# Prompt attentions with one more unit in flight, and output projection weights loaded a stage ahead with longer weight rings

## The chip, the cores and the metric

The kernel runs on one core of a Trainium2 chip. The metric is the device time of one execution in microseconds (us); lower is better. TensorE is called PE here, VectorE DVE, ScalarE ACT, GpSimd POOL and SyncE SP.

## The reference

One decode step of a two-layer decoder, all float32, for a prompt of 256 tokens and 8 sample sequences of 8 tokens each (320 tokens in all, width 1024). Layer 0 mixes by latent attention and dilated window attention, layer 1 by a gated convolution; each layer then attends to a memory and runs a sparse expert layer ("peer"). Cut to what matters:

```
x <- LN(a*x + mixer(x));  x <- LN(a*x + mem_attend(x));  x <- LN(a*x + PEER(x))

def mla_attend(q_pos, q_lat, q_rope, ckv, krope, k_pos):
    s = (einsum(q_lat, ckv) + einsum(q_rope, krope)) * MLA_SCALE      # 8 heads, 256 + 32 features
    p = softmax(where(k_pos <= q_pos, s, -inf)); return einsum(p, ckv)
o_mla = einsum(o_lat, w_uv)                                            # w_uv: 256 x 8 x 64
# window attention: 3 groups of 4 heads of 128; bias = rel_bias[bucket(distance)], softmax, weighted sum
y = concat([o_mla, o_swa]) @ attn_w_out                                # layer 0
y = (b_gate * conv(c_gate * h)) @ conv_w_out                           # layer 1
def mem_attend(x, kv, wq, wo):                                         # 256 memory rows, 4 heads of 256
    s = einsum(x @ wq, k) * MEM_SCALE; return einsum(softmax(s), v) @ wo
```

## The kernel before

The program is a row of stages. Each stage is one `k.block()` (line 182), and all engines meet at its end, so a stage that ends earlier starts the next one earlier. Intermediate results stay in SBUF. SP issues nearly all transfers, on one queue, in the order in which its program has them. Names of tiles begin with the name of their stage.

The stages that the prediction speaks of, in order of time:

- **mlp** (100.6 to 207.2 us): `attend_prompt`, latent attention of the prompt. 16 units of one head and one block of 128 queries: units 0 to 7 have 128 keys, 8 to 15 have 256. The object `BiasByDistance` (lines 1250 to 1290) works beside it: in units 3 to 10 PE makes the window attention's bias by distance (L1281, 15 products with 33 rows and 4 columns of weights), ACT takes them (L1288), and when all 15 are taken SP stores them (L1269) and spreads each of the three groups over 128 rows of DRAM (L1273, 3 transfers of 1 MB).
- **ms** set-up and **mls**: the sample's latent attention. A small stage loads the page table and a mask (L1472, L1473) and waits for both; then `attend_sample` reads page numbers from the table and loads pages.
- **mv** (448.0 to 467.0 us), `mla_values_stage`: loads `w_uv` (0.5 MB, L1224), then 32 matmuls (L1232).
- **swp** (682.5 to 741.5 us): `attend_prompt`, window attention of the prompt; 8 units, 4 with 384 score columns, 4 with 768.
- **nx0** and **nx1**, **nm0** and **nm1**, **nf0**: `joined_stage`. It runs a list of products in units of two weight chunks (1024 x 512, 2 MB each) through a ring of two slots. In nx0 and nx1 the first unit is the mixer's output projection; then a layer norm of the residual runs on DVE while PE makes the memory's keys or values; x is turned (L441) after a given chunk (after chunk 3 in nx0, after chunk 2 in nx1), and the memory queries follow. nm0 and nm1 have the memory's output projection alone.
- **m0p** and **m1p** (44.1 and 44.6 us): `attend_prompt`, memory attention of the prompt; 8 units of 256 keys. Then **m0s** and **m1s**, the sample's, which stream 1 MB pieces of the memory cache.
- **c_**: `odd_mixer`, the convolution on DVE, between nf0 and nx1.
- **peer** (p0e, p1e): about 815 us each; not touched.

In `attend_prompt` one unit passes through these steps: scores on PE (L664), bias or copy, maximum and scale on DVE (L700 or L703, L705, L706: `maxima`), exponential on ACT (L735), division on DVE (L712, L713: `finish`), transposes on PE (L673), their copy to `pT` on ACT (L747), the product with the values on PE (L679), and its copy out on DVE (L719: `take`). Scores have two PSUM buffers; `pT` has one. The orders are written out by hand:

```
PE,  unit u:  scores(u+1); bias products; transposes(u), wait for pT, values(u)
DVE, unit u:  finish(u); maxima(u+1); take(u)
ACT, unit u:  exps(u+1); bias copies; copy of pT(u)
```

So between the transposes of unit u and its values PE waits until ACT has done `exps(u+1)`, which itself waits for `maxima(u+1)`, and the copy.

In `joined_stage` a chunk's load waits until the chunk two before it is done (`wait(sp, chunk_done, n - 1)`), and PE waits before chunk n for its weights and for `bank_free >= n - 1`, the evacuation of chunk n - 2. With 320 tokens the last 64 are computed for both chunks of a unit together, so both chunks are done, and can be evacuated, only at the unit's end.

Of the kernel before, what the change touches and what calls it, by code (L numbers as in the profile page):

```python
# [16 lines left out]
P = 128  # L17
# [88 lines left out]
class Kernel:  # L106


    def __init__(self, nc, ctx, io):
# [5 lines left out]
        self.window_stored = ctx.enter_context(nc.semaphore("window_stored"))  # L115
        self.mem_kv_stored = ctx.enter_context(nc.semaphore("mem_kv_stored"))
# [221 lines left out]
def joined_stage(k, name, out_job, norm, mid=(), last=(), turn_at=0, memT=None):  # L338
# [12 lines left out]
    with ExitStack() as ctx:  # L351
        ring = k.sb(ctx, name + "_w", [P, 2, KC * 512])
# [4 lines left out]
        w_landed = [k.sem(f"{name}_w_landed{s}") for s in range(2)]  # L357
# [14 lines left out]
        def slot_view(s, kc, chunk):  # L372
            return ring[:, s, 0:kc * chunk].rearrange("p (c n) -> p c n", c=kc)

        @block.sync
        def _(sp):
            def load(n):
                (_, aT, w, chunk, _), i = units[n // 2]
                src = w[:, (2 * i + n % 2) * chunk:(2 * i + n % 2 + 1) * chunk].rearrange("(c p) n -> p c n", p=P)
                wait(sp, chunk_done, n - 1)  # L380
                sp.dma_start(slot_view(n % 2, aT.shape[1], chunk), src).then_inc(w_landed[n % 2], 16)
# [9 lines left out]
            for n in range(2 * len(units)):  # L391
                load(n)
                if n == 1 and out_job:
                    load_norm()

        @block.tensor
        def _(pe):
            def product(u, between):
# [3 lines left out]
                for s in range(2):  # L402
                    n = 2 * u + s
                    pe.wait_ge(w_landed[s], 16 * (u + 1))
                    wait(pe, bank_free, n - 1)
                    wv = slot_view(s, kc, chunk)
# [14 lines left out]
                if paired:  # L421
                    j, (t0, rows) = len(parts(kind, aT, chunk)) - 1, parts(kind, aT, chunk)[-1]
                    for c in range(kc):
                        for s in range(2):
                            mm = pe.matmul(k.ps[64 * s:64 * s + 64, 4 * s + j, 0:chunk], aT[:, c, t0:t0 + rows],
                                           slot_view(s, kc, chunk)[:, c, :], start=(c == 0), stop=(c == kc - 1))
# [201 lines left out]
def attend_prompt(k, name, units, cols, scale, mask_scales, beside=None):  # L628
# [3 lines left out]
    with ExitStack() as ctx:  # L632
        s = k.sb(ctx, name + "_s", [P, 2, cols])
        p = k.sb(ctx, name + "_p", [P, 2, cols])
        pT = k.sb(ctx, name + "_pT", [P, cols // P, P])
# [23 lines left out]
        def _(pe):  # L659
# [8 lines left out]
            def values(u):  # L668
# [5 lines left out]
                mm.then_inc(turned, 1)  # L674
                pe.wait_ge(pT_ready, u + 1)
                wait(pe, o_taken, u - 1)
                for b in range(len(units[u]["outs"])):
                    for j, (_, vs) in enumerate(keys):
                        mm = pe.matmul(k.ps[:, 6 + u % 2, b * P:(b + 1) * P], vs[b], pT[:, j, :],  # L679
                                       start=(j == 0), stop=(j == len(keys) - 1))  # L680
                mm.then_inc(o_ready, 1)

            scores(0)
            for u in range(U):
                if u + 1 < U:
                    scores(u + 1)
                if beside:
                    beside.tensor(pe, u)
                values(u)

        @block.vector
        def _(dve):
# [30 lines left out]
            for u in range(U):  # L723
# [3 lines left out]
                take(u)  # L727

        @block.scalar
        def _(act):  # L730
# [20 lines left out]
def attend_sample(k, name, a):  # L751
# [7 lines left out]
    with ExitStack() as ctx:  # L759
# [32 lines left out]
        def _(sp):  # L792
# [27 lines left out]
            repeat_ends(sp, PAIRS, body)  # L820

# [392 lines left out]
def mla_values_stage(k, e):  # L1214

    nc, io = k.nc, k.io
    with ExitStack() as ctx:
        wuv = k.sb(ctx, "mv_wuv", [P, 2, MLA_H, D_V])
        landed, made, taken = k.sem("mv_landed"), k.sem("mv_made"), k.sem("mv_taken")
        block = ctx.enter_context(k.block())  # L1220

        @block.sync
        def _(sp):
# [152 lines left out]
def even_mixer(k, oT):  # L1376
# [3 lines left out]
    with ExitStack() as ctx:  # L1380
        e = {"oT": oT}
        with ExitStack() as c1:
# [6 lines left out]
            e["mask"] = k.sb(c1, "e_causal", [P, 2, SEQ])  # L1389
            with ExitStack() as c2:  # L1390
# [61 lines left out]
def mla_sample(k, e):  # L1452
    nc, io = k.nc, k.io
    with ExitStack() as ctx:
# [10 lines left out]
        half = PAST // 2  # L1465
        table_landed, masked = k.sem("ms_table_landed"), k.sem("ms_masked")
        with ExitStack() as c2:
# [196 lines left out]
def memory_attention(k, memory):  # L1664
# [790 lines left out]
```

## Time and profile before

| | |
|---|---|
| median of 3 runs | 3481.22 us (3477.48 to 3485.13) |
| the profiled execution | 3498.17 us |
| its span | 3496.4 us |
| busy share PE / DVE / ACT / POOL | 84% / 43% / 16% / 18% |
| prompt attention stages mlp, swp, m0p, m1p | 106.6, 59.0, 44.1, 44.6 us |
| the two peer stages | about 1630 us together |

The profile has one execution: busy time of each engine, the span in 40 slices with TensorE's granted clock in tenths of full speed, groups of instructions by line, and which wait ended each idle time. A window "A:B" is counted in us from the span's start. A matmul of float32 shows two records for each instruction, so "x8" in a row of matmuls is four instructions.

### The profile page before, as it was taken

The page shows a single profiled execution, that of the slowest core. Times are in us where ns is not written, and L with a number is a line of the kernel's source. Part 1 is how long each engine was busy: PE and PEld are TensorE (multiplying, and loading weights), DVE is VectorE, ACT ScalarE, POOL GpSimd, SP SyncE. Part 2 cuts the span into 40 slices and gives each one's busy share as a digit, 9 for nine tenths or more (in the row PEclk, how much of TensorE's full clock was granted, in tenths as well). Part 3 has the DMA queues.
Part 4 walks back from the last instruction along what each step waited for, and adds up shares of the span by engine and source line. Part 5 has one row for each costly group of instructions (what it writes and reads, how often), then busy time and mean ns, then how long its engine had stood idle before and what let it go on. Part 6 is the DMA issues. An engine that isn't in the chain of part 4 may idle for free. (4 is left out here: it accounts for less than half of the span.)

```text
span 3496.4 us, 45163 instructions
## 1 busy us (share of the span) xinstructions
PE 2934.1 (84%) x17313; PEld 2381.8 (68%) x17313; DVE 1509.9 (43%) x3598; ACT 544.2 (16%) x1380; POOL 612.4 (18%) x642
## 2 busy tenths in 40 slices
PE   6867768866669668999989998968678999999997
PEld 3434423554535438999989997644437999989997
DVE  1211100022210225997975553021215997985553
ACT  1223300133301211112100000101221112110000
POOL 0000040000000000433443330000000432443330
PEclk8668889878889789999999999989698999999998
DMA  3349977859842433998989996322343898989995
GB/s 116 108 148 300 316 206 253 280 158 244 206 160 96 162 115 122 355 378 305 348 311 409 409 409 215 121 86 96 121 156 122 318 381 300 349 310 409 408 409 210
DMA packets 275160, 867.70 MB, mean 248 GB/s; under 512 B 30625, under 2 KB 54210, under 8 KB 272423
## 3 DMA queue, kind: packets, MB, share of 16 engines
q1 hardware_dynamic: 198932, 593.14, 48.6%
q0 software_dynamic: 76032, 271.88, 20.6%
q8 instruction: 130, 2.13, 0.3%
q14 instruction: 66, 0.54, 0.0%
HBM read 846.23 MB, written 109.08 MB: 273 GB/s over the span
## 5 line engine op out<-in xcount | busy, mean ns | idle before, releaser
L2271 PE MATMUL ps<-xT,p0e_uT 128*128 128x192 f32 x2048 | 345.9, 328 | 11.1 <-DMA p0e_uT<-in_peer_uT 6.7
L2271 PE MATMUL ps<-xT,p1e_uT 128*128 128x192 f32 x2048 | 345.7, 328 | 9.5 <-DMA p1e_uT<-in_peer_uT 6.4
L2271 PEld LDWEIGHTS ps<-xT,p0e_uT 128*128 128x128 f32 x2048 | 334.0, 191 | 13.9 <-DMA p0e_uT<-in_peer_uT 8.4
L2297 PE MATMUL ps<-p0e_S,p_qT 128*128 128x192 f32 x2048 | 337.3, 327 | 6.3 <-DMA p_qT<-in_peer_v 6.3
L2271 PEld LDWEIGHTS ps<-xT,p1e_uT 128*128 128x128 f32 x2048 | 334.7, 191 | 11.6 <-DMA p1e_uT<-in_peer_uT 7.8
L2297 PE MATMUL ps<-p1e_S,p_qT 128*128 128x192 f32 x2048 | 337.2, 327 | 5.6 <-DMA p_qT<-in_peer_v 5.4
L2297 PEld LDWEIGHTS ps<-p0e_S,p_qT 128*128 128x128 f32 x2048 | 333.1, 190 | 10.4 <-DMA p_qT<-in_peer_v 10.4
L2297 PEld LDWEIGHTS ps<-p1e_S,p_qT 128*128 128x128 f32 x2048 | 332.4, 190 | 10.1 <-DMA p_qT<-in_peer_v 10.0
L2075 DVE SCALAR_TENSOR_TENSOR h_tok<-p1e_rows,p1e_dots,h_tok 128x1024 f32<-128x1024 f32 x127 | 163.1, 1284 | 143.7 <-DMA p1e_rows<-in_peer_v,p1e_expert 125.7
L2075 DVE SCALAR_TENSOR_TENSOR h_tok<-p0e_rows,p0e_dots,h_tok 128x1024 f32<-128x1024 f32 x127 | 163.1, 1284 | 141.3 <-DMA p0e_rows<-in_peer_v,p0e_expert 134.5
L1965 POOL DMA_INDIRECT p0e_rows<-in_peer_u,p0e_expert x128 | 153.4, 1199 | 394.7 <-DVE p0e_dots L2064 207.1
L1965 POOL DMA_INDIRECT p1e_rows<-in_peer_u,p1e_expert x128 | 153.4, 1199 | 393.9 <-DVE p1e_dots L2064 206.9
L1965 POOL DMA_INDIRECT p1e_rows<-in_peer_v,p1e_expert x128 | 127.0, 992 | 195.2 <-DVE h_tok L2075 172.7
L1965 POOL DMA_INDIRECT p0e_rows<-in_peer_v,p0e_expert x128 | 126.1, 985 | 196.4 <-DVE h_tok L2075 174.7
L2064 DVE CUSTOM_DVE_ANT_0 p1e_rows<-p1e_rows,x_tok 128x1024 f32<-128x1024 f32 x128 | 154.9, 1218 | 1.6
L2064 DVE CUSTOM_DVE_ANT_0 p0e_rows<-p0e_rows,x_tok 128x1024 f32<-128x1024 f32 x128 | 154.9, 1218 | 1.6
L844 PE MATMUL ps<-ident,ms_pages 128*128 128x128 f32 (+1 forms) x384 | 70.3, 340 | 64.9 <-DMA ms_pages<-in_cache_mla 60.3
L503 DVE SCALAR_TENSOR_TENSOR x_tok<-x_tok,h_tok 128x1024 f32<-128x1024 f32 (+1 forms) x15 | 17.4, 1218 | 236.9 <-ACT h_tok L471 195.9
L293 PE MATMUL ps<-win_w,xT 128*128 128x512 f32 x192 | 89.9, 630 | 29.3 <-DMA win_w<-in_attn_w_in 29.3
L700 DVE SCALAR_TENSOR_TENSOR swp_s<-ps,e_bias_p 128x384 f32<-128x384 f32 (+1 forms) x8 | 6.1, 757 | 241.2 <-PE ps L664 241.2
L844 PEld LDWEIGHTS ps<-ident,ms_pages 128*128 128x128 f32 (+1 forms) x384 | 48.1, 155 | 86.7 <-DMA ms_pages<-in_cache_mla 37.6
L2288 PE MATMUL ps<-h_tok 128*128 128x128 f32 x768 | 102.6, 276 | 3.3 <-DVE h_tok L2085 3.3
(460 smaller groups left out, 3991.2 us busy)
## 6 DMA issues: line engine op xcount, KB each, us to landing
p_qT<-in_peer_v SPq DMA_DIRECT2D x256, 512.0 KB
p0e_uT<-in_peer_uT SPq DMA_DIRECT2D x128, 512.0 KB
p1e_uT<-in_peer_uT SPq DMA_DIRECT2D x128, 512.0 KB
out_swa_sample<-in_cache_swa_w SPq DMA_DIRECT2D x32, 2040.0 KB, 18.7
m_cache<-in_cache_mem_kv SPq DMA_DIRECT2D x32, 1024.0 KB, 5.8
ms_pages<-in_cache_mla SPq DMA_DIRECT2D x128, 144.0 KB, 2.6
ss_kcache<-in_cache_swa_w SPq DMA_DIRECT2D x72, 256.0 KB, 9.2
ss_vcache<-in_cache_swa_w SPq DMA_DIRECT2D x72, 256.0 KB
```

The costliest lines, as they stand in the source:

```text
L293: mm = pe.matmul(k.ps[0:rows, 4 * s + j, 0:chunk], aT[:, c, t0:t0 + rows], wv[:, c, :], start=(c == 0), stop=(c == kc - 1))
L503: dve.scalar_tensor_tensor(out=k.x[0:n, i, :], in0=k.x[0:n, i, :], scalar=ALPHA, in1=k.h[0:n, i, :], op0=ALU.mult, op1=ALU.add).then_inc(c ...
L700: dve.scalar_tensor_tensor(out=dst, in0=src, scalar=mask_scales, in1=units[u]["bias"], op0=ALU.mult, op1=ALU.add).then_inc(s_read, 1) \
L844: mm = pe.transpose(k.ps[0:w, bank(0, g, slot, G), j * P:(j + 1) * P], src(slot), k.ident[:, :])
L1965: pool.indirect_dma_start(out=gr[:, n % NG, :], out_offset=None, in_=io[table].rearrange("l e d -> (l e) d"), in_offset=bass.IndirectOffse ...
L2064: dve.tensor_tensor_reduce(out=gr[:, n % NG, :], in0=gr[:, n % NG, :], in1=k.x[:, 0, :], scale=1.0, scalar=0.0, op0=ALU.mult, op1=ALU.add, ...
L2075: dve.scalar_tensor_tensor(out=acc, in0=gr[:, (HK + n) % NG, :], scalar=dots[:, n:n + 1], in1=acc, op0=ALU.mult, op1=ALU.add).then_inc(row ...
L2271: mm = pe.matmul(k.ps[:, SB[i % len(SB)], 0:TD], ur[:, i % NU, c, :], k.xT[:, c, D0:T], start=(c == 0), stop=(c == KC - 1))
L2288: mm = pe.matmul(k.ps[:, spread_bank(G), m * P:(m + 1) * P], hotJ[:, G % 2, m, :], hotI[:, G % 2, m, :], start=True, stop=True)
L2297: mm = pe.matmul(k.ps[:, c // 2, c % 2 * TD:(c % 2 + 1) * TD], vr[:, i % NV, c * P:(c + 1) * P], S[:, i, :], start=False, stop=(i == STEPS ...
```

## The change

The prompt attentions keep one more unit in flight: scores of two units ahead are made first, the values of unit u - 1 come before the transposes of unit u, `pT` has two buffers, and ACT copies `pT(u)` before `exps(u+1)`. The weight rings become objects (`Ring`) that can live across stages: nx0 gets 4 slots, nx1 3 (its ring is also used by nf0), nm0 and nm1 keep 2. The two chunks of the memory's output projection are loaded by SP at the end of m0s and m1s, those of the convolution's in `odd_mixer`. `w_uv` is loaded in the ms set-up stage.

```diff
@@ -335,7 +337,29 @@
+class Ring:
+    def __init__(self, k, ctx, name, slots):
+        self.k, self.slots, self.ahead = k, slots, 0
+        self.tile = k.sb(ctx, name + "_w", [P, slots, KC * 512])
...
+    def load_ahead(self, sp, job):
+        self.k.n_ahead += 16
+        self.ahead = self.k.n_ahead
+        for n in range(2):
+            self.load(sp, n, job, 0).then_inc(self.k.w_ahead[n], 16)
...
-                wait(sp, chunk_done, n - 1)
-                sp.dma_start(slot_view(n % 2, aT.shape[1], chunk), src).then_inc(w_landed[n % 2], 16)
+                job, i = units[n // 2]
+                wait(sp, chunk_done, n - NR + 1)
+                ring.load(sp, n, job, i).then_inc(w_landed[n % NR], 16)
...
-            for n in range(2 * len(units)):
+            if first:
+                load_norm()
+            for n in range(first, 2 * len(units)):
...
-        pT = k.sb(ctx, name + "_pT", [P, cols // P, P])
+        pT = k.sb(ctx, name + "_pT", [P, 2, cols // P, P])
...
             scores(0)
+            scores(1)
             for u in range(U):
-                if u + 1 < U:
-                    scores(u + 1)
+                if u > 0:
+                    values(u - 1)
+                turn(u)
+                if u + 2 < U:
+                    scores(u + 2)
                 if beside:
                     beside.tensor(pe, u)
-                values(u)
+            values(U - 1)
...
                 finish(u)
                 if u + 1 < U:
                     maxima(u + 1)
-                take(u)
+                if u > 0:
+                    take(u - 1)
+            take(U - 1)
...
             exps(0)
             for u in range(U):
+                act.wait_ge(turned, u + 1)
+                wait(act, o_ready, u - 1)
+                nk = len(units[u]["keys"])
+                act.activation(pT[:, u % 2, 0:nk, :].rearrange("p a b -> p (a b)"), psf[:, 2048:2048 + nk * P],
+                               ACT.Copy).then_inc(pT_ready, 1)
                 if u + 1 < U:
                     exps(u + 1)
                 if beside:
                     beside.scalar(act, u)
-                act.wait_ge(turned, u + 1)
-                wait(act, o_ready, u)
-                nk = len(units[u]["keys"])
-                act.activation(pT[:, 0:nk, :].rearrange("p a b -> p (a b)"), psf[:, 2048:2048 + nk * P],
-                               ACT.Copy).then_inc(pT_ready, 1)
...
+            if a.get("ahead"):
+                a["ahead"](sp)
...
-            sp.dma_start(wuv[:, :, :, :], io["mla_w_uv"][0].rearrange("(c p) h n -> p c h n", p=P)).then_inc(landed, 16)
...
-            pe.wait_ge(landed, 16)
...
-                sp.wait_ge(table_landed, 32)
+                sp.dma_start(wuv[:, :, :, :], io["mla_w_uv"][0].rearrange("(c p) h n -> p c h n", p=P)).then_inc(table_landed, 16)
+                sp.wait_ge(table_landed, 48)
...
+                "ahead": lambda sp: ring.load_ahead(sp, memory.out),
...
+                ring.load_ahead(sp, out_job)
```

In the diff the pieces stand in the order of the file: `joined_stage` (from `wait(sp, chunk_done, ...)`), `attend_prompt` for PE, DVE and ACT (from `pT = ...`), `attend_sample` for SP (`a.get("ahead")`), `mla_values_stage`, the ms set-up, `memory_attention` and `odd_mixer`.

PE in m0p, first units, before and in the changed kernel (L664 and L694 are scores, L673 and L703 transposes, L679 and L712 values):

```order
L664 MATMUL ps<-m_kT,m_qT 128x256 x4
L673 MATMUL ps<-ident,m0p_p 128x128 x2
L679 MATMUL ps<-m0p_pT,m_mkv 128x128 x4
L664 MATMUL ps<-m_kT,m_qT 128x256 x2
L673 MATMUL ps<-ident,m0p_p 128x128 x2
L679 MATMUL ps<-m0p_pT,m_mkv 128x128 x4
```

```order
L694 MATMUL ps<-m_kT,m_qT 128x256 x4
L703 MATMUL ps<-ident,m0p_p 128x128 x2
L694 MATMUL ps<-m_kT,m_qT 128x256 x2
L712 MATMUL ps<-m0p_pT,m_mkv 128x128 x4
L703 MATMUL ps<-ident,m0p_p 128x128 x2
L694 MATMUL ps<-m_kT,m_qT 128x256 x2
L712 MATMUL ps<-m0p_pT,m_mkv 128x128 x4
```

Between a unit's transposes and its values now stands the next scores product; before, the values followed their transposes directly.

SP at the end of m0s and the start of nm0, before and changed:

```order
L1699 DMA m_cache<-in_cache_mem_kv 128x2x1024 x3
L182 UNCONDITIONAL_BRANCH
L181 ISA
L375 UNCONDITIONAL_BRANCH
L381 DMA nm_w<-in_mem_wo 128x8x512 x2
L385 DMA nm_gain<-in_ln_mem_g 128x1024
L385 DMA nm_shift<-in_ln_mem_b 128x1024
```

```order
L1738 DMA m_cache<-in_cache_mem_kv 128x2x1024 x3
L353 DMA nm_w<-in_mem_wo 128x8x512 x2
L184 UNCONDITIONAL_BRANCH
L183 ISA
L401 UNCONDITIONAL_BRANCH
L410 DMA nm_gain<-in_ln_mem_g 128x1024
L410 DMA nm_shift<-in_ln_mem_b 128x1024
```

The two weight loads stand before the stage's end and before the gain and shift, right behind the last cache loads.

## Rows read from the trace of the kernel before

**Rows 1.** Windows: length; busy PE, PEld, DVE, ACT, POOL; PEclk, DMA share, GB/s.
```profile
100.60:207.20 106.60, 90.11 (x246) 49.91 (x246) 27.95 (x113) 21.42 (x64) 0.00 (x0) 0.53 0.32 115
682.50:741.50 59.00, 35.55 (x180) 32.27 (x180) 20.37 (x48) 11.34 (x24) 0.14 (x1) 0.68 0.26 71
1138.20:1182.30 44.10, 28.32 (x112) 22.02 (x112) 15.28 (x56) 8.24 (x25) 0.11 (x1) 0.68 0.12 48
```

**Rows 2.** Timeline of m0p: start us, us, engine, line, what, [idle before <-releaser].
```profile
1141.60 0.44 PE L673 MATMUL ps<-ident,m0p_p 128*128 128x128 f32 x2 [1.51 <-DVE m0p_p L713]
...
1143.48 1.94 PE L679 MATMUL ps<-m0p_pT,m_mkv 128*128 128x128 f32 x8 [1.44 <-ACT m0p_pT L747]
...
1145.21 1.91 PE L664 MATMUL ps<-m_kT,m_qT 128*128 128x256 f32 x4
...
1145.86 0.15 DVE L712 RECIPROCAL m0p_stat<-m0p_stat 128x1 f32<-128x1 f32 x1
...
1146.92 0.46 PE L673 MATMUL ps<-ident,m0p_p 128*128 128x128 f32 x2
...
1147.16 0.42 DVE L703 COPY m0p_s<-ps 128x256 f32<-128x256 f32 x1 [0.76 <-PE ps L664]
...
1148.27 0.51 ACT L735 ACTIVATE m0p_p<-m0p_s,m0p_stat 128x256 f32<-128x256 f32 x1 [4.84 <-DVE m0p_stat L706]
...
1149.19 1.16 PE L679 MATMUL ps<-m0p_pT,m_mkv 128*128 128x128 f32 x8 [1.81 <-ACT m0p_pT L747]
```

**Rows 3.** Timeline of swp, a unit with 768 columns.
```profile
720.39 0.96 DVE L700 SCALAR_TENSOR_TENSOR swp_s<-ps,e_bias_p 128x768 f32<-128x768 f32 x1 [1.54 <-PE ps L664]
...
724.34 2.93 PE L679 MATMUL ps<-swp_pT,e_kv 128*128 128x128 f32 x12 [3.24 <-ACT swp_pT L747]
```

**Rows 4.** Timeline of SP: bias store, its spreading, the page table's load.
```profile
171.67 0.28 SPq L1269 DMA_DIRECT2D scratch_bias_by_dist<-bs_by_dist  x1
177.12 15.41 SPq L1273 DMA_DIRECT2D scratch_bias_rep<-scratch_bias_by_dist  x3
207.21 0.24 SPq L1472 DMA_DIRECT2D ms_table<-in_page_table  x1
```

**Rows 5.** Windows around the end of mlp, and POOL's first instruction of mls.
```profile
205.00:210.00 5.00, 1.26 (x6) 0.97 (x5) 0.55 (x3) 0.00 (x0) 0.00 (x0) 0.50 0.27 102
...
211.00:212.00 1.00, 0.00 (x0) 0.00 (x0) 0.00 (x0) 0.00 (x0) 0.00 (x0) 0.50 0.05 17
```

**Rows 6.** Timeline: start of mls, then mv's first matmul.
```profile
212.66 0.29 POOL L1497 COPY ms_q<-e_qlatT 128x128 f32<-128x128 f32 x1 [112.09 <-POOLq L182]
...
459.45 7.01 PE L1232 MATMUL ps<-e_olatT,mv_wuv 128*64 128x320 f32 x32 [12.12 <-DMA mv_wuv<-in_mla_w_uv]
```

**Rows 7.** Waits of PE for weights in nx0, nm0 and nx1: us, times, longest.
```profile
PE ps L413 <- DMA nx_w<-in_mem_wk: 7.9, 1, 7.9
...
PE ps L413 <- DMA nm_w<-in_mem_wo: 8.4, 1, 8.4
...
PE ps L413 <- DMA nx_w<-in_conv_w_out: 22.2, 1, 22.2
```

**Rows 8.** Timeline, joined stages: evacuation, chunk at full clock, SP, values, x_tok, turning.
```profile
1029.75 3.13 ACT L471 ACTIVATE h_tok<-ps 128x512 f32<-128x512 f32 x6 [63.06 <-PE ps L425]
...
2190.96 14.00 PE L413 MATMUL ps<-nf_w,m_memT 128*128 128x512 f32 x32
...
2331.65 1.03 SPq L381 DMA_DIRECT2D nx_w<-in_conv_w_out  x2
...
2384.77 16.34 PE L413 MATMUL ps<-nx_w,m_memT 128*128 128x512 f32 x32 [7.78 <-DMA nx_w<-in_mem_wv]
...
2396.75 1.22 DVE L533 TENSOR_TENSOR x_tok<-x_tok,nx_shift 64x1024 f32<-64x1024 f32 x1
...
2400.95 1.04 PE L441 MATMUL ps<-ident,x_tok 128*128 128x128 f32 x8
```

**Rows 9.** Windows: the first peer stage.
```profile
1335.00:2150.00 815.00, 794.17 (x5004) 782.66 (x5003) 581.98 (x1356) 79.59 (x279) 279.46 (x256) 0.99 0.88 333
```

More of the change, by code:

```diff
@@ L115, in __init__ @@
         self.window_stored = ctx.enter_context(nc.semaphore("window_stored"))
+        self.w_ahead = [ctx.enter_context(nc.semaphore(f"w_ahead{n}")) for n in range(2)]
+        self.n_ahead = 0
         self.mem_kv_stored = ctx.enter_context(nc.semaphore("mem_kv_stored"))
@@ L356, in joined_stage @@
         rstd = k.sb(ctx, name + "_rstd", [P, 3])
-        w_landed = [k.sem(f"{name}_w_landed{s}") for s in range(2)]
+        NR = ring.slots
+        w_landed = [k.sem(f"{name}_w_landed{s}") for s in range(NR)]
         chunk_done, bank_free = k.sem(name + "_chunk_done"), k.sem(name + "_bank_free")
@@ L370, in parts, with loads_of_slot @@
             return list(range(chunk // P))
-        def slot_view(s, kc, chunk):
-            return ring[:, s, 0:kc * chunk].rearrange("p (c n) -> p c n", c=kc)
+        first = 2 if ring.ahead else 0
+        def loads_of_slot(n):
+            return sum(1 for m in range(first, n + 1) if m % NR == n % NR)
         @block.sync
@@ L403, in product @@
                     n = 2 * u + s
-                    pe.wait_ge(w_landed[s], 16 * (u + 1))
+                    if n < first:
+                        pe.wait_ge(k.w_ahead[n], ring.ahead)
+                    else:
+                        pe.wait_ge(w_landed[n % NR], 16 * loads_of_slot(n))
                     wait(pe, bank_free, n - 1)
-                    wv = slot_view(s, kc, chunk)
+                    wv = ring.view(n, kc, chunk)
                     for j, part in enumerate(parts(kind, aT, chunk)):
@@ L425, in product @@
                             mm = pe.matmul(k.ps[64 * s:64 * s + 64, 4 * s + j, 0:chunk], aT[:, c, t0:t0 + rows],
[L426 removed]
+                                           ring.view(2 * u + s, kc, chunk)[:, c, :], start=(c == 0), stop=(c == kc - 1))
                             if c == kc - 1:
@@ L666, in scores, with turn @@
                 mm.then_inc(scored, 1)
-            def values(u):
+            def turn(u):
                 pe.wait_ge(p_ready, u + 1)
@@ L674, in values @@
                 mm.then_inc(turned, 1)
+            def values(u):
+                keys = units[u]["keys"]
                 pe.wait_ge(pT_ready, u + 1)
@@ L1733, in memory_attention, with odd_mixer @@
             })
-def odd_mixer(k, prod, cT):
+def odd_mixer(k, prod, cT, ring, out_job):
     nc, io = k.nc, k.io
@@ L2359, in decode_step @@
             memory = Memory(k, c1, 0)
-            joined_stage(k, "nx0", ("tok", oT, io["attn_w_out"][0], 512, k.h), norm_of["mix"][0],
-                         mid=[memory.keys, memory.values], last=[memory.queries], turn_at=2, memT=memory.T)
-            memory_attention(k, memory)
-            joined_stage(k, "nm0", memory.out, norm_of["mem"][0])
+            with ExitStack() as c2:
+                joined_stage(k, "nx0", Ring(k, c2, "nx0", 4), ("tok", oT, io["attn_w_out"][0], 512, k.h), norm_of["mix"][0],
+                             mid=[memory.keys, memory.values], last=[memory.queries], turn_at=2, memT=memory.T)
+            ring = Ring(k, c1, "nm0", 2)
+            memory_attention(k, memory, ring)
+            joined_stage(k, "nm0", ring, memory.out, norm_of["mem"][0])
         peer(k, 0)
@@ L2366, in decode_step @@
             memory = Memory(k, c1, 1)
[L2367 to L2375 removed]
+            with ExitStack() as c2:
+                cT = k.sb(c2, "c_convT", [P, 8, T])
+                ring = Ring(k, c2, "nx1", 3)
+                conv_out = ("tok", cT, io["conv_w_out"][0], 512, k.h)
+                with ExitStack() as c3:
+                    prod = k.sb(c3, "c_prod", [P, 24, T])
+                    joined_stage(k, "nf0", ring, None, norm_of["ffn"][0], mid=[memory.keys],
+                                 last=[("feat", k.xT, io["conv_w_in"][0], 512,
+                                        prod[:, :, :].rearrange("p a t -> p (a t)"))],
+                                 turn_at=1, memT=memory.T)
+                    odd_mixer(k, prod, cT, ring, conv_out)
+                joined_stage(k, "nx1", ring, conv_out, norm_of["mix"][1],
+                             mid=[memory.values], last=[memory.queries], turn_at=1)
+            ring = Ring(k, c1, "nm1", 2)
+            memory_attention(k, memory, ring)
+            joined_stage(k, "nm1", ring, memory.out, norm_of["mem"][1])
         peer(k, 1)
```

32 lines of the change are left out of this document (13 added, 19 removed).

## The prediction

> **What bounds the kernel now.** The windows by stage come first. The first peer stage keeps PE busy for 794 of 815 us at a clock of 0.99 [rows 9], and nothing here touches it or its twin. The change works in the other half, where PE waits. The prompt attentions are the worst of it: in m0p PE is busy for 28.3 of 44.1 us, in swp for 35.6 of 59.0, at a mean clock of 0.68, in mlp for 90.1 of 106.6 at 0.53 [rows 1]. Next, the timeline of m0p shows why. In every unit PE idles between transposes and values, 1.44 or 1.81 us, released by ACT's copy to `pT` (L747) [rows 2]: ACT takes `exps(u+1)` first, which waits for DVE. In swp that idle is 3.3 us per unit [rows 3]. The rest are waits at stage starts: for `w_uv` 12.12 [rows 6], and for weights 7.9, 8.4 (alike in nm1) and 22.2 [rows 7].
>
> All sums go against the profiled execution, 3498.2 us, which is 17.0 us (0.5%) above the median.
>
> **Memory attentions (m0p, m1p).** After T(0) at 1141.6 the new order leaves 6 scores, 8 values, 7 transposes. At the low clock values start 1.73 before the next scores, these 1.71 before the transposes, and the transposes take 0.44 to 0.46 [rows 2]. If PE alone bounds, 6 x 1.71 + 8 x 1.73 + 7 x 0.44 = 27.2, with 1.1 for the last copy out: end at 1169.9 instead of 1182.3, -12. At the full clock values take 1.16 [rows 2], and another loop bounds: `finish` (reciprocal at 1145.86 until DVE idles at 1147.16 - 0.76) 0.54, `maxima` (1147.16 to the exponential at 1148.27) 1.11, the exponential 0.51 [rows 2], and 0.2 of handing over, 2.35 a unit. T(7) then comes 7 x 2.35 after 1141.6, and 2.3 later the stage ends, 1160.4: -22. The granted clock is one of two levels, 1.2 or 2.4 GHz; a mean of 0.68 is a mixture, and the full level comes in m0p where scores, transposes and values followed each other without idle from 1143.48 on [rows 2]. The new order removes the idles, so I take mostly high clock, **-18 each, -36**.
>
> The low clock has a rule behind it too: the Trainium skill ("TensorE: Matmul & The Clock Gate", A second HAM failure mode: psum-queue depth-cycling) says that frequent short idles between groups of matmuls make the clock go to and fro, with throughput lost between bursts. By it the chain-bound order would defeat itself, with -12 for each of the two stages; the trace agrees as far as 0.68 is a mixture [rows 1], and that is the second case below.
>
> **Window attention (swp).** PE-bound: 35.6 busy [rows 1] and some 5 of start and end, 41: -18. Chain-bound: 4 units with 768 columns (bias addition 0.96 [rows 3]; by the same steps 4.06) and 4 with 384 (2.8), 27.4, and 4.1 before: -27. **-22.**
>
> **Latent attention (mlp).** PE idles 16.5 us there [rows 1], and I expect little of it. The bias tables leave late: store at 171.67, then the spread, whose three issues take until 192.5; the page table's load is issued at 207.21 [rows 4] on the same queue, behind them. DMA share is 0.27 up to 210 and 0.05 from 211 [rows 5], so the table lands only when the spread ends, and mls starts at 212.66 [rows 6]. What counts is thus when the last bias product is made, not when mlp ends; and the new PE order puts scores of unit 12 and transposes of 10 ahead of bias(10), 3.4 us of low-clock work against 6 to 8 of idle removed before it. So bias comes some 3 earlier at the low clock. `w_uv`, 0.5 MB, now joins this set-up's wait: 1.5 to 2 more. From +1 (low clock, nothing won) to -25 (full clock from unit 3 on); nearer to the low end, since the stage's clock is 0.53, **-6**.
>
> The share of 0.27 is about 4 of 16 DMA engines. The Trainium skill ("DMA: Bandwidth & Descriptors", Why a DMA increments its semaphore by 16 and not by 1) has it that a transfer uses the largest number of engines, up to 16, that divides its slowest dimensions, the lowest-numbered ones, and so the page table's one row would go by an engine that the spread uses too. The trace agrees with it in the share of 0.27 [rows 5]; which engine the table's load uses, no row shows. By this rule the term is -6, without it rival 3.
>
> **mv.** The 12.12 for `w_uv` [rows 6] goes; the load's cover is the whole of mls. PE starts with the clock as mls left it, so -11 to -13: **-12.5**.
>
> **nx0, four slots.** The load of chunk n waits for chunk n - 4 and no longer n - 2, so that for `mem_wk` runs beside the output projection and its wait of 7.9 [rows 7] goes. Late next: `bank_free` for chunk 0, half of ACT's 3.13 us of evacuation [rows 8], since chunks 0 and 1 end together: 1.6. That is -6.3, and the chunk behind it keeps its clock: 32 records take 16.34 after an idle and 14.00 without [rows 8], of which I take 1.7. Bounds 7 and 8.5. **-8.**
>
> **nm0, nm1.** The loads now stand behind the last cache load on SP's queue (order above), 4 MB which land some 2 us into the stage, so 7.5 of 8.4 [rows 7] go, and the start is warm, 2 more at most. Behind them the gain and shift, not wanted before the product's end. 7.5 to 9.7 each: **-9.5 each, -19**.
>
> **Convolution into nx1.** SP issued the weights at 2331.65 [rows 8] and PE waited 22.2 [rows 7], up to 2339.4. Loaded in `odd_mixer` they are there at the start: PE starts at 2331.7, -7.7. The convolution's state stores queue behind 4 MB, hidden by DVE's convolution, which ends only with the stage. If that cover were gone, they would hold the stage by some us. Then the values: their wait of 7.78 [rows 8] turns into the same 1.6 for evacuation. But the turn after chunk 2 asks for `x_tok`, and DVE's last norm row starts at 2396.75, ready at 2398.0, 3.0 before the turn at 2400.95 [rows 8], so only 5 of the 6.2 are kept: 3.5 to 6. **-12.7.**
>
> nf0 has three slots but no wait for weights of over 1 us to lose, the peer stages and sample attentions do not change: 0.
>
> **Sum:** -36 - 22 - 6 - 12.5 - 8 - 19 - 12.7 = **-116**, 3382 for a profiled execution; less the 17 between it and the median, **3365**.
>
> **Rivals.**
> 1. *The low or flickering clock.* Everything in the attentions is PE-bound: -12 x 2, -18, 0 in mlp, and starts at the low clock (mv -11, nx0 -7, nm -15, nx1 -9): -84, 3397. For it: half of m0p ran low [rows 1, 2], and chain-bound units leave PE idle for over 0.5 us each. Against it: the longest idles, all over 1.4 us [rows 2], go.
> 2. *The full clock throughout,* the bias products too: -22 x 2, -27, -25, and the upper ends elsewhere, -149: 3332. Against it: mlp's 0.53 though PE was busy 85% of the time [rows 1].
> 3. *The spread does not hold the page table.* Then the idle of mlp pays directly: of 16.5 [rows 1] some 5 are the stage's start and end, so mlp ends about 11 earlier, at 196, and mls starts 3 later, at 199 instead of 212.66 [rows 6]: -13.7 instead of -6, 3357. Against it: 0.27 falls to 0.05 just before POOL's start [rows 5, 6].
> 4. *Loads ahead bring nothing*, since the queue holds them up until where they land now, and longer rings wait for banks: half of the 52 outside the attentions goes, 3391.
> 5. *Slower.* The peer stages run at 0.99 [rows 9] beside DMA at 0.88 share and DVE at 71%. If the chip grants less to a program that works denser before them, each us at 1.2 instead of 2.4 GHz costs up to half a us: to undo 116 some 232 of the 1630 us would have to go low, a mean clock of 0.93. Over that point the kernel is slower than 3488. The trace has no sign of such a link.
>
> A measurement of this kernel tells about 0.2% (7 us) from no change.
>
> **How the numbers follow.** Forecast 0.50; rival 1 0.27, 2 0.10, 3 0.08, 4 0.03, slower 0.02. The forecast with its terms half-way to rival 1's and rival 2's is -100 to -132, 3381 to 3349. The range goes to rival 2 on one side and rival 1 on the other, 3334 to 3400, which leaves out rival 5 and the tails of 1 and 2, less than 0.2. All cases but the fifth are faster by over 2%: faster 0.97, same 0.01, slower 0.02.
>
> **What the changed profile would show.** In m0p, units 2.4 to 3.9 us apart, no idle of PE before values released by L747, and a clock above 0.8 (below 0.6 for rival 1). In mlp, the last ACT copy of bias (L1288) at about 168 and POOL's first copy in mls at about 206; at about 195, rivals 2 or 3. mv's first matmul within 1 us of the stage's start. In nx0 one idle of 1.6 released by ACT. In nm0 and nm1 waits under 1 us. In nx1 the turn (L441) waiting for DVE. Peer stages of 815 us as before. The prediction is wrong in its reasons if PE still waits in swp for `pT`, if the wait for `mem_wk` is over 3, or if mls starts before the DMA share falls; wrong in its size if the attentions give less than 42 together.

## The result, and the profile after

The changed kernel takes 3348.64 us (median of 4 runs, 3338.0 to 3356.41), the kernel before 3483.18 beside it: a ratio of 0.9611, interval 0.9576 to 0.9645. Timed once more with the experiments below, it was 0.963 (0.960 to 0.966). So it is 3.9% faster, 134.5 us; 116 were forecast, and the range of 3334 to 3400 holds the time. The profiled execution took 3352.74 us, its span is 3350.9.

First the windows of the changed kernel, in the columns of [rows 1]: mlp, swp, m0p, then the first peer stage.

```profile
100.40:175.10 74.70, 63.96 (x246) 38.47 (x246) 29.39 (x113) 21.82 (x65) 0.10 (x1) 0.73 0.41 145
...
660.30:691.70 31.40, 22.77 (x180) 20.39 (x180) 19.83 (x48) 12.15 (x24) 0.06 (x1) 1.00 0.49 134
...
1059.50:1081.20 21.70, 18.17 (x112) 15.00 (x112) 14.80 (x56) 8.97 (x25) 0.12 (x1) 1.00 0.24 98
...
1206.40:2050.10 843.70, 811.67 (x5118) 798.56 (x5118) 582.00 (x1357) 84.61 (x293) 277.93 (x256) 0.99 0.87 330
```

Read length, PE busy and clock together. m0p went from 44.1 to 21.7 us; 10.2 of these 22.4 are PE's own work, done at the full clock (28.32 to 18.17), 12.2 are idle time. The clock is 1.00 in both short stages. The peer stage is as it was: it takes some 842 us in the kernel before too, of which the 815 of [rows 9] are only the stretch that was looked at (the two together take 1681 us, not 1630).

A unit of m0p in the timeline of the changed kernel:

```profile
1066.61 0.16 DVE L749 RECIPROCAL m0p_stat<-m0p_stat 128x1 f32<-128x1 f32 x1 [0.27 <-ACT m0p_p L774]
...
1067.08 0.42 DVE L740 COPY m0p_s<-ps 128x256 f32<-128x256 f32 x1
...
1067.21 0.44 PE L703 MATMUL ps<-ident,m0p_p 128*128 128x128 f32 x2
...
1067.49 1.03 PE L694 MATMUL ps<-m_kT,m_qT 128*128 128x256 f32 x4
...
1068.17 0.51 ACT L774 ACTIVATE m0p_p<-m0p_s,m0p_stat 128x256 f32<-128x256 f32 x1
...
1068.35 1.05 PE L712 MATMUL ps<-m0p_pT,m_mkv 128*128 128x128 f32 x8
...
1068.80 0.17 DVE L749 RECIPROCAL m0p_stat<-m0p_stat 128x1 f32<-128x1 f32 x1 [0.27 <-ACT m0p_p L774]
```

From one reciprocal to the next are 2.19 us: 0.47 to the next `maxima`, 1.09 of it, 0.63 of exponential. DVE and ACT bound the stage now; the values (L712) have no idle ahead of them in this unit, the scores of the unit after next stand where PE waited.

Then SP in the changed kernel around the end of mlp, its wait there, POOL's first copy of mls, and the windows in which the spread runs out (to be read against [rows 4] to [rows 6]):

```profile
152.85 0.28 SPq L1305 DMA_DIRECT2D scratch_bias_by_dist<-bs_by_dist  x1
158.31 15.98 SPq L1309 DMA_DIRECT2D scratch_bias_rep<-scratch_bias_by_dist  x3
175.17 8.73 SPq L1510 DMA_DIRECT2D ms_table<-in_page_table  x1
...
184.57 0.57 SPq L1512 DMA_DIRECT2D e_wuv<-in_mla_w_uv  x1
```

```profile
SPq L184 <- DMA e_wuv<-in_mla_w_uv: 9.3, 1, 9.3
```

```profile
194.89 0.29 POOL L1536 COPY ms_q<-e_qlatT 128x128 f32<-128x128 f32 x1 [94.09 <-POOLq L184]
```

```profile
165.00:175.00 10.00, 0.72 (x7) 0.53 (x5) 0.49 (x2) 0.00 (x0) 0.00 (x0) 0.68 0.26 101
176.00:184.00 8.00, 0.00 (x0) 0.00 (x0) 0.00 (x0) 0.00 (x0) 0.00 (x0) 0.50 0.26 102
```

The bias store comes 18.8 us earlier than in [rows 4], and mls starts 17.8 earlier than in [rows 6]. PE is done with mlp by 166, then no engine computes for 29 us: the spread goes on at a DMA share of 0.26, and from 175 on the set-up's three loads are issued behind it. SP itself is held in issuing the spread until 174.3, and with it the end of the stage.

Next, mv and the first product of win in the changed kernel, and for win the same row of before:

```profile
428.46 4.55 PE L1268 MATMUL ps<-e_olatT,e_wuv 128*64 128x320 f32 x32 [0.65 <-PEq L184]
453.60 2.08 PE L295 MATMUL ps<-win_w,xT 128*128 128x512 f32 x2 [20.59 <-DMA win_w<-in_attn_w_in]
```

```profile
477.55 2.93 PE L293 MATMUL ps<-win_w,xT 128*128 128x512 f32 x3 [11.09 <-DMA win_w<-in_attn_w_in]
```

The idle of 12.12 before mv's first matmul [rows 6] is gone, but the next stage's first wait for weights has grown from 11.09 to 20.59 (17.65 in a second profile).

Next, PE's waits in the changed kernel that answer to [rows 7], nx0's and nx1's evacuation, the turn in nx1, and the memory's output weights in nm0 and nm1 together:

```profile
PE ps L443 <- ACT h_tok L501: 1.7, 1, 1.7
...
PE ps L471 <- DVE x_tok L563: 2.1, 1, 2.1
...
PE ps L443 <- DMA nm_w<-in_mem_wo: 4.1, 2, 2.6
```

Last, PE's waits in swp, for `pT` before and in the changed kernel, then for the divided exponentials (`swp_p`):

```profile
PE ps L679 <- ACT swp_pT L747: 19.4, 8, 3.3
```

```profile
PE ps L703 <- DVE swp_p L750: 6.1, 7, 2.1
...
PE ps L712 <- ACT swp_pT L782: 1.8, 2, 0.9
```

The wait for `pT` is gone but for two of 0.9 us in the last two units, where no scores are left to stand in the gap.

By stages, in us, from two profiles of each kernel (the second of before is the experiment x_before, the second of after is after_again, the changed kernel run once more):

| | before | after | forecast |
|---|---|---|---|
| start of mls | 212.7, 210.7 | 194.9, 195.3 | -6 |
| mv | 19.6, 18.6 | 5.7, 5.7 | -12.5 |
| win up to swp | 215.3, 214.8 | 226.5, 221.8 | 0 |
| swp | 58.9, 58.4 | 31.4, 31.5 | -22 |
| sws | 241.0, 214.4 | 219.9, 222.0 | 0 |
| nx0 | 155.7, 155.4 | 147.7, 147.4 | -8 |
| m0p, m1p | 44.1, 44.7; 44.5, 41.8 | 21.8 in all four | -18 each |
| nm0, nm1 | 67.8, 67.3; 67.2, 67.2 | 60.4, 61.4; 60.3, 62.4 | -9.5 each |
| nx1 | 127.2, 127.4 | 113.9, 113.4 | -12.7 |
| peer stages, both | 1680.7, 1674.6 | 1686.4, 1683.6 | 0 |

### The profile page after: what moved, and what is told of

The parts are those of the page before. It is cut to its first block and busy times, and to the rows that moved or that the text cites. A ratio compares the mean times of both kernels' runs of the same rounds, so it can differ in the third digit from the quotient of the medians.

```text
span 3350.9 us, 45159 instructions
## 1 busy us (share of the span) xinstructions
PE 2865.4 (86%) x17313; PEld 2338.8 (70%) x17313; DVE 1509.8 (45%) x3598; ACT 545.6 (16%) x1380; POOL 607.6 (18%) x642
## 3 DMA queue, kind: packets, MB, share of 16 engines
q0 software_dynamic: 76032, 271.88, 21.5%
## 5 line engine op out<-in xcount | busy, mean ns | idle before, releaser
L446 PE MATMUL ps<-xT,nx_w 128*128 128x320 f32 x640 | 172.8, 432 | 0.0
L446 PEld LDWEIGHTS ps<-xT,nx_w 128*128 128x128 f32 x640 | 121.6, 190 | 51.6 <-issue 1.4
L443 PE MATMUL ps<-nx_w,m_memT 128*128 128x512 f32 x256 | 115.6, 612 | 19.1 <-DMA nx_w<-in_mem_wk 15.6
```

The lines of the kernel that those rows point to most:

```text
L443: mm = pe.matmul(k.ps[0:rows, 4 * s + j, 0:chunk], aT[:, c, t0:t0 + rows], wv[:, c, :], start=(c == 0), stop=(c == kc - 1))
L446: mm = pe.matmul(k.ps[:, 4 * s + j, 0:aT.shape[2]], wv[:, c, j * P:(j + 1) * P], aT[:, c, :], start=(c == 0), stop=(c == kc - 1))
```

## The experiments

**x_before.** No edit. One row did not fit: sws, untouched, seemed 21 us shorter after.

> The kernel before, unchanged, profiled a second time. Open is where 21 us of the window attention's sample stage (sws) went: 240.9 us in the profile of before, 219.9 in the profile after, with no edit in it. Theory A (a hiccup of that one execution: DMA shares fall to 0.6 to 0.8 at every turn of its loop after one idle of PE put down to issue): sws takes 220 to 230 here, and the span is 10 us or more below 3496. Theory B (the stage before hands sws a state that makes it slow): sws takes 238 to 243 again, the span stays at 3490 to 3500.

Measured: sws 214.4 us, span 3448.1: theory A, with sws even below its 220 to 230. The windows of sws, first profile of before, then x_before:

```profile
741.50:982.40 240.90, 159.90 (x2024) 114.85 (x2024) 51.63 (x104) 89.84 (x160) 4.38 (x17) 0.84 0.89 229
```

```profile
736.10:950.50 214.40, 152.33 (x2024) 107.61 (x2024) 51.64 (x104) 89.86 (x160) 4.34 (x17) 0.89 0.93 257
```

The same instructions at 229 and at 257 GB/s. Over the 14 profiles of this study sws lies between 212.5 and 241.0 and both peer stages together between 1675 and 1689, with no relation to an edit. So 26 of the 48 us between the two spans of one kernel are this stage, and a stage of that kind is not read from a single pair. The kernel before itself had a median of 3483.18 us beside the changed kernel and of 3463.86 beside x_before, so runs of different occasions are compared by their ratios to it.

**act_swap.** The changed kernel, with

```diff
             scores(0)
-            scores(1)
             for u in range(U):
-                if u > 0:
-                    values(u - 1)
-                turn(u)
-                if u + 2 < U:
-                    scores(u + 2)
+                if u + 1 < U:
+                    scores(u + 1)
                 if beside:
                     beside.tensor(pe, u)
-            values(U - 1)
+                turn(u)
+                values(u)
...
-                if u > 0:
-                    take(u - 1)
-            take(U - 1)
+                take(u)
```

> The changed kernel, with PE and DVE in the old order of the units and ACT alone in the new one (copy of pT(u) ahead of exps(u+1)). Theory A (what cost the time was ACT's order; a unit more in flight gives the rest): PE waits 0.5 to 0.7 us before each values product, DVE's finish(u+1) comes behind take(u), a unit of m0p takes 3.3 us at the full clock, m0p 29 us, m1p 29, swp about 43, mls starts some 5 us later than in the changed kernel: 28 to 38 us slower than the changed kernel, about 3380. Rival (without a unit more in flight the idles keep the clock at the low level): m0p and m1p 36 to 40 us, swp 50, mls starts 10 or more later: 55 to 70 slower, about 3410.

Measured: m0p and m1p 28.2, swp 34.7, mls starts at 214.8; ratio 0.9714 (0.9669 to 0.9758). m0p in its window and one of its values products, then mlp:

```profile
1084.50:1112.70 28.20, 19.86 (x112) 14.31 (x112) 14.78 (x56) 9.04 (x25) 0.14 (x1) 1.00 0.18 75
```

```profile
1095.03 1.16 PE L712 MATMUL ps<-m0p_pT,m_mkv 128*128 128x128 f32 x8 [0.47 <-ACT m0p_pT L777]
```

```profile
101.00:165.00 64.00, 60.05 (x144) 29.04 (x144) 17.04 (x71) 13.80 (x43) 0.10 (x1) 0.50 0.41 146
171.00:188.00 17.00, 13.66 (x75) 9.42 (x74) 9.12 (x34) 5.08 (x16) 0.00 (x0) 1.00 0.19 49
```

Theory A's sizes came out in m0p (29 said), and swp was better than said (43). ACT's order alone brings 16 of the 22.5 us of m0p, 24 of 27 in swp, and the full clock; the idle of 0.47 us that it leaves before each values product does not cost the clock. But mlp was far off: mls was to start 5 us later, it starts 20 later. The total, 36 us over the changed kernel by the ratios, lies within theory A's 28 to 38 only because the 8 us better in swp offset more than half of the 15 us worse in mlp. PE stayed at the low clock from 101 until 169.4. In the changed kernel:

```profile
100.40:130.00 29.60, 29.18 (x86) 17.84 (x86) 11.45 (x48) 8.59 (x27) 0.10 (x1) 0.50 0.88 315
134.80:165.00 30.20, 29.25 (x146) 17.42 (x145) 16.52 (x58) 11.99 (x34) 0.00 (x0) 1.00 0.08 17
```

it had no idle between units and ran at the full clock from 134.4 on, with 6 of the 15 bias products made. The 7th is the first of unit 6 and comes at 134.81, against 136.42 in act_swap and 137.00 in the kernel before: up to there, at the low clock, the new order is ahead by 1.6 and 2.2 us. Then from this product to the last one, the same instructions, in the changed kernel, in act_swap and in the kernel before:

```profile
134.81:151.80 16.99, 16.99 (x72) 8.33 (x71) 7.94 (x28) 7.75 (x20) 0.00 (x0) 1.00 0.00 0
```

```profile
136.42:170.45 34.03, 32.35 (x71) 13.84 (x70) 7.30 (x28) 6.75 (x20) 0.00 (x0) 0.52 0.00 0
```

```profile
137.00:169.57 32.57, 30.47 (x72) 13.74 (x71) 7.31 (x28) 7.65 (x20) 0.00 (x0) 0.55 0.00 0
```

So of the 20 us by which the bias store comes earlier than in act_swap (152.85 against 172.63), 17 arise behind the 7th product. PE idles only 1.7 us of them in act_swap; the other 15 are the clock. The extra unit in flight goes with most of mlp's gain, and ACT's order alone brought nothing to the start of mls. Why the level rose so much earlier is not shown.

**old_order.** act_swap with ACT's old order too:

```diff
             for u in range(U):
-                act.wait_ge(turned, u + 1)
-                wait(act, o_ready, u - 1)
...
                 if u + 1 < U:
                     exps(u + 1)
                 if beside:
                     beside.scalar(act, u)
+                act.wait_ge(turned, u + 1)
+                wait(act, o_ready, u)
...
```

> The changed kernel with the old order on PE, DVE and ACT; rings, early loads and w_uv stay as changed. Theory A (terms add up): m0p and m1p 44 to 45 us, swp 59, mls starts at about 213 or 214: 90 us slower than the changed kernel, about 3438. If sws becomes slow with it (theory B above), 21 more: 3459. Rival (the ahead loads and rings gain only because the attentions run at the full clock): over 3465.

Measured: ratio 0.988 (0.9818 to 0.9942); mls starts at 212.2, swp 54.7, m0p 44.4, m1p 44.5. The stages give 17.1 + 23.3 + 45.3 = 85.7 us of loss, near the 90 of theory A, and sws stays at 212.5, so its addition from theory B falls. With 0.9611 for the changed kernel the ratios give 0.027, some 94 us.

**attn_only.** The other way round: the kernel before, with the new `attend_prompt` alone.

> The kernel before with the new order in the prompt attentions alone (two buffers of pT, PE, DVE and ACT as changed); rings, w_uv and the loads of weights as before. Theory (terms add up, as undoing them showed): mls starts 16 to 19 us earlier, swp 31.5 instead of 58.5, m0p and m1p 21.8 instead of 44.5: 86 to 92 us faster than the kernel before, ratio 0.973 to 0.976. Rival (part of the gain in the attentions needs the other half of the change): under 70 us, ratio above 0.98.

Measured: ratio 0.9683 (0.9638 to 0.9727); mls starts at 193.5, swp 31.4, m0p and m1p 21.8; nx0 155.1 and nm0 67.0 as before, nx1 125.3, which is 2 under before. Its stages sum to 18.2 + 27.2 + 44.0 = 89.4 us, as the theory has it; the ratio gives 110 and its interval ends at 95, just past what was expected. The sign and the rank are settled (the attentions are 70% of the whole gain by the stages and by old_order, 80% by this ratio); the other 20 us can lie in the scatter of stages with no edit, which is not shown.

**wuv_back.** The changed kernel, with

```diff
-                sp.dma_start(wuv[:, :, :, :], io["mla_w_uv"][0].rearrange("(c p) h n -> p c h n", p=P)).then_inc(table_landed, 16)
-                sp.wait_ge(table_landed, 48)
+                sp.wait_ge(table_landed, 32)
...
+        @block.sync
+        def _(sp):
+            sp.dma_start(wuv[:, :, :, :], io["mla_w_uv"][0].rearrange("(c p) h n -> p c h n", p=P)).then_inc(landed, 16)
...
+            pe.wait_ge(landed, 16)
```

> The changed kernel with w_uv loaded in mv_values_stage again. Theory A (the wait was for the backlog of copies issued in mls, which the win stage's first weights meet next, and the load holds the set-up of mls): set-up 16 us instead of 19.7, mv 19 instead of 5.7, win 215 instead of 220 to 226; in total 3 to 6 us slower than the changed kernel. Rival, as predicted (a stall of 12.12 us removed and nothing late behind it): 12 to 14 slower.

Measured: set-up 18.6 instead of 19.7, mv 18.2 instead of 5.7, win 214.2 instead of 221.8 in the run beside it. Its PE rows:

```profile
442.48 6.57 PE L1273 MATMUL ps<-e_olatT,e_wuv 128*64 128x320 f32 x32 [11.13 <-DMA e_wuv<-in_mla_w_uv]
...
460.65 14.59 PE L295 MATMUL ps<-win_w,xT 128*128 128x512 f32 x30 [11.61 <-DMA win_w<-in_attn_w_in]
```

The wait of 11 is back in mv and win's first is 11.6 again: -1.1 + 12.5 - 7.6 = 3.8 us. The two spans agree (3343.5 and 3343.3); the medians (3356.76 and 3346.10) have overlapping intervals and decide nothing. Theory A holds by the stages: most of the stall moved by one stage. But win alone took 221.8 and 226.5 us in two profiles of the changed kernel, so the net of this edit is between nothing and 4 us.

**nx0_two** and **nm_late**, a profile of each: in nx0 `Ring(k, c2, "nx0", 2)` for 4; and the line `"ahead": lambda sp: ring.load_ahead(sp, memory.out)` left out.

> The changed kernel with two slots instead of four in nx0's ring. Theory (as predicted): PE waits 7.9 us for mem_wk again and the product behind it starts at the low clock; nx0 155 to 156 us instead of 147.5, 8 slower. Rival (x_tok's norm or the turn bounds nx0, the ring does not): nx0 within 2 of 147.5.

> The changed kernel without the early loads of mem_wo (nm0 and nm1 load both chunks themselves). Theory (as predicted, the wait of 8.4 us goes by loading ahead): PE waits 8 to 8.5 us for mem_wo in both, nm0 and nm1 67 to 68 us instead of 60.4 and 62, 12 to 14 us in all. Rival (the cache loads' own transfers end later too, so the wait only moves): m0s and m1s 2 us or more shorter, under 8 us in all.

Measured: nx0 155.2 us, and the waits for `mem_wk` (nx0_two) and `mem_wo` (nm_late):

```profile
PE ps L443 <- DMA nx_w<-in_mem_wk: 8.2, 1, 8.2
```

```profile
PE ps L443 <- DMA nm_w<-in_mem_wo: 17.0, 2, 8.5
```

nm0 is 67.7 and nm1 67.9. The four slots are worth 7.8, the early loads of `mem_wo` 7.3 and 6.0, as the theories said. The third load ahead, the convolution's output weights in nx1, was not undone by a run of its own: attn_only, which lacks it, has nx1 at 125.3 and the changed kernel at 113.7, so it is worth some 12 us.

**spread16.** The spread written with 128 rows outermost:

```diff
-            src = bass.AP(io["bias_by_dist"].tensor, g * SWA_H * N_DIST + REP0, [[N_DIST, SWA_H], [0, P], [1, REP_N]])
-            sp.dma_start(io["bias_rep"][g], src).then_inc(k.bias_spread, 16)
+            src = bass.AP(io["bias_by_dist"].tensor, g * SWA_H * N_DIST + REP0, [[0, P], [N_DIST, SWA_H], [1, REP_N]])
+            sp.dma_start(io["bias_rep"][g].rearrange("h p n -> p h n"), src).then_inc(k.bias_spread, 16)
```

> The changed kernel with the transfers that spread the bias written with the 128 rows outermost, and the 4 heads inside; the same bytes. Theory A (the start of mls waits for these transfers, which run on 4 of 16 DMA engines and land 40 us after the store): DMA share in the spread rises from 0.27 to near 1, SP issues them in under 6 us, the stage mlp ends with its matmuls at about 167, POOL's first copy in mls comes at 171 to 175 instead of 194.9; total 15 to 24 us faster than the changed kernel. Rival 1 (mls and win are bound by the copies' transfers, so that an earlier start is given back there): start as said, but total under 8 us faster. Rival 2 (the page table is late for another reason): start unchanged at 190 to 195.

Measured: ratio 0.9595 (0.9546 to 0.9645), POOL's first copy at 177.0. SP and the DMA share in it, and the same window of the changed kernel:

```profile
153.12 0.28 SPq L1305 DMA_DIRECT2D scratch_bias_by_dist<-bs_by_dist  x1
158.57 1.95 SPq L1309 DMA_DIRECT2D scratch_bias_rep<-scratch_bias_by_dist  x3
166.93 0.24 SPq L1510 DMA_DIRECT2D ms_table<-in_page_table  x1
```

```profile
160.00:170.00 10.00, 5.04 (x33) 3.61 (x31) 3.57 (x14) 1.74 (x6) 0.00 (x0) 0.94 0.97 259
```

```profile
160.00:170.00 10.00, 4.78 (x31) 3.57 (x30) 3.50 (x13) 1.47 (x6) 0.00 (x0) 0.93 0.24 87
```

Three issues take 1.95 us instead of 15.98, the share is 0.97 instead of 0.24, and mls starts 17.9 us earlier (at 177.0, where 171 to 175 was said). That shows what the prediction only inferred, that mls waited for a narrow transfer. Nothing of it is given back up to swp, which starts at 638.4 against 660.1 and 656.3 in the two profiles of the changed kernel, so rival 1 falls for these stages. The gain in the whole, 0.0016 to 0.0035 of the ratio or 6 to 12 us, is unclear: no changed kernel was timed beside it.

**hoist.** spread16, with the table, the mask and w_uv loaded by `BiasByDistance.sync` ahead of the zeros (tiles kept in `e`, set-up without a load):

```diff
+        sp.dma_start(self.e["ms_table"][:, :], io["page_table"].rearrange("b n -> (b n)").unsqueeze(0)).then_inc(self.early, 16)
+        sp.dma_start(self.e["ms_mask"][0:64, :], io["causal_new"]).then_inc(self.early, 16)
+        sp.dma_start(self.e["wuv"][:, :, :, :], io["mla_w_uv"][0].rearrange("(c p) h n -> p c h n", p=P)).then_inc(self.early, 16)
         k.copy_some(sp, 16)
+        sp.wait_ge(self.early, 48)
```

> spread16 with the page table, its mask and w_uv loaded in the latent attention's stage, ahead of the copies of zeros, so that mls needs no transfer that is issued behind the spread. Theory A (set-up waits only for transfers behind the spread): set-up under 2 us instead of 10.1, POOL's first copy in mls at 168 to 169 instead of 177.0; SP's first page loads still queue behind what is left of the spread up to 175, so PE's first matmul of mls comes 5 to 8 earlier than in spread16: total 4 to 8 us faster than spread16, 20 to 30 faster than the changed kernel. Rival (page loads, not the table, are what the spread holds up): PE's first matmul of mls at the same time as in spread16, no gain over it.

Measured: POOL's first copy at 167.85, PE's first matmul of mls at 182.05 instead of 191.36 in spread16; ratio 0.9542 (0.9498 to 0.9586) where the changed kernel beside it has 0.963 (0.960 to 0.966), 22 us by the medians and 31 by the ratios, as theory A said. It holds at the start of mls too (9.2 us). mls took 234.5 as ever, but win 227.5 where spread16 has 221.8, so of the 9 us over spread16 some 3 are there at swp; win's own scatter is as large as this loss.

**copies_late.** The changed kernel, with

```diff
-COPY_ROWS, COPIED_IN_LOOP = 510, 3
+COPY_ROWS, COPIED_IN_LOOP = 510, 2
...
+                if n < len(copies):
+                    k.copy_some(sp, copies[n])
...
+                             copies=(0, 0, 0, 0, 0, 2, 2, 4))
```

> The changed kernel with two instead of three copies of 2 MB per sequence in the mls loop, and the other eight issued in nx0 after its weight loads, where the DMA share is 0.35. Theory A (mls and the first weights of win wait for DMA engines that the copies fill: share 0.87 in mls, first wait of win 18 to 22 us): mls 205 to 218 us instead of 233 to 238, win's first wait 11 us or less and win 212 to 218 instead of 222 to 226, nx0 and m0p within 3 us of now: 20 to 35 us faster than the changed kernel, ratio to the kernel before 0.952 to 0.957. Rival 1 (mls is bound by its page loads and PE's 168 us of work, the copies only fill gaps): mls over 228. Rival 2 (the eight copies hold up mem_wv, mem_wq or the output of m0p): nx0 or m0p 8 us or more longer, no gain.

Measured: mls 225.7 us, win 216.1, nx0 147.3, ratio 0.9553 (0.9521 to 0.9585). Its windows of mls and win, and its first wait in win:

```profile
192.30:418.10 225.80, 170.20 (x1296) 106.75 (x1296) 41.91 (x120) 75.83 (x136) 5.73 (x32) 0.86 0.72 233
423.70:639.80 216.10, 172.97 (x517) 87.70 (x518) 0.00 (x0) 17.81 (x39) 36.90 (x57) 0.91 0.77 257
```

```profile
PE ps L295 <- DMA win_w<-in_attn_w_in: 29.6, 5, 11.7
```

By the ratios that is 20 to 27 us under the changed kernel. win answered as theory A had it (first wait 11.7 instead of 20.59 and 17.65), mls only by 8 of the 15 to 28 expected: its share fell from 0.87 to 0.72 while its length hardly moved, so the copies are not most of what bounds it; what does was not tried. The eight copies cost nx0 nothing: 147.3 us, as without them.

**best.** hoist and copies_late together.

> copies_late and hoist together: spread over all DMA engines, table and w_uv loaded early, eight copies moved to nx0. Theory: the two gains add up, since one shortens the start of mls and the other its length: 45 to 60 us faster than the changed kernel, ratio to the kernel before 0.943 to 0.949. Rival (mls ends when the same transfers have drained, so an earlier start is given back): no more than 10 us faster than copies_late.

Measured: 3306.84 us (3297.51 to 3311.66), ratio 0.9494 (0.9478 to 0.951): the fastest kernel here, 5.1% under the one before and 1.2 to 1.4% (41 to 47 us) under the changed one by the ratios, at or just short of the low end of the 45 to 60 expected. It is 20 us under copies_late, timed beside it, where the rival allowed 10. mls starts at 167.5, takes 226.6, win 214.2.

## Why the prediction was right, and where it was off

**What bounds.** Right. PE's idle between transposes and values came from ACT's order: ACT's order alone (act_swap) removes most of it in m0p and swp. The prediction named as a sign against its reasons that PE still waits in swp for `pT`: 1.8 of 19.4 us are left, in the last two units.

**Memory attentions, -18 each.** Mechanism right, size at the far end of its bounds: -22.5 in m0p. The step that undersized it is "I take mostly high clock": it was the full clock in every unit (1.00), with a unit at 2.19 us where 2.35 were worked out. The Trainium skill ("TensorE: Matmul & The Clock Gate", A second HAM failure mode: psum-queue depth-cycling) has frequent short idles between groups of matmuls make the clock oscillate. In these stages that did not come: PE idles in every unit or nearly so, in swp up to 2.1 us at a time, and both stay at 1.00. The old order, with 1.4 to 3.3 us in every unit, goes with 0.65 to 0.76. The length of the idles does not order all cases, though: mlp before had only 0.43 us a unit between its first bias products and ran at 0.53. **swp, -22:** -27, for the same reason.

**mlp, -6.** The chain was right (last bias product, spread, page table: start of mls moved by 17.8 with a store 18.8 earlier), its term was three times too small. Its bound for the low clock was good ("some 3 earlier": 2.2 up to unit 6). The failed step is "nearer to the low end, since the stage's clock is 0.53": the clock of a stage under the old order was taken for the new one. The level rose at 134.4 (139.1 in a second profile) and the bias products from unit 6 to the last took 17.0 us instead of 32.6, of which 13.5 are the clock and 2.1 idle time. act_swap shows the other branch, the low clock until 169.4 and nothing gained. The prediction said that POOL's first copy at about 195 would mean rival 2 or 3: it came at 194.9, and it is rival 2's way, the full clock. Rival 3 fell: mls began only when the share of 0.26 had ended (at about 193). The Trainium skill ("DMA: Bandwidth & Descriptors", Why a DMA increments its semaphore by 16 and not by 1) has the number of engines follow from the slowest dimension; spread16 agrees, 0.24 with 4 heads outermost and 0.97 with 128 rows. Which engine the table's load takes, no run shows.

**mv, -12.5.** The failed step is "the load's cover is the whole of mls", with nothing late next. The wait was not for w_uv's own transfer but for what was queued ahead of it; win's weights met the rest. That this was the copies issued in mls is supported by copies_late, where fewer of them bring win's first wait back to 11.7. The net of mv and win is 4.3 us by the means of the table, and 3.8 by wuv_back, within win's scatter.

**nx0, -8** and **nx1, -12.7:** right, 8.0 and 13.7, with the late-next waits as named (1.7 for ACT, 2.1 for `x_tok`); nx1's part was not undone by a run. **nm0 and nm1, -9.5 each:** 7.1 and 5.4. The weights still are 1.5 and 2.6 us late, and the warm start did not come: PE's busy time in nm0 is 41.50 us after and 42.05 before, at a granted clock of 0.80 and 0.79. What was taken for clock there was not.

**Rivals.** Rivals 1 and 2 bracketed the total: the attentions went by rival 2 (-22, -27; mlp part of the way), the memory's outputs by rival 1, mv stayed even below it, and nx0 and nx1 went as forecast. The peer clock is 0.99 and 0.98, so the slower case had nothing. By the means of the table the attentions gave 24 us more than forecast (16.6 + 27.2 + 22.5 + 21.5 = 88 against 64), mv with win and the memory's outputs 15 less. So the total was nearer than its parts, which is luck: two terms of the wrong size, with nothing in common, partly cancelled. (Rival 2's own terms add up to 151, not 149; nothing hangs on it.) The stages sum to 126; the medians' 134.5 has some 8 more, which the scatter of the untouched stages can hold.

## What to carry to other kernels

When a stall goes, follow the resource that it waited for, not the consumer: a backlog on the DMA queue meets the next stage's first load. Find the one transfer whose outermost dimension is small before rearranging the work around it. Where TensorE's clock is mixed, cost a new order at both levels as bounds, and do not carry the old order's mean over.

## What was not expected of the hardware

In mlp of the changed kernel PE was busy for 29.18 of 29.60 us and still ran at the low level. The level rose at 134.4, 2.2 us after the start of unit 8's scores, the first with 256 keys; but in after_again, the same kernel, it rose at 139.1, 10.0 us after them, so these scores are not the sign. In the ten profiles with the new order it rose 32 to 39 us after the start of the stage. In act_swap, whose units had only short idles of some 0.4 us, it did so 68 us after the start, and in the kernel before first after 60, for 3.4 us. In m0p and swp, with PE idle for 16 and 27% of the time, the full level held throughout. What orders these cases was not tried. And one kernel's two profiles differ by 48 us of span, 26 of them in one stage that streams by DMA.
